# Angle steps and half of the phase tables on GpSimd, kernel rows by DMAs within SBUF

## The reference, cut to what matters

```python
dt = jnp.exp(log_dt)[:, None]                        # 32 groups, 64 states each
mag = jnp.exp(a_re * dt)
ab_re, ab_im = mag * jnp.cos(a_im * dt), mag * jnp.sin(a_im * dt)
inv = 1.0 / (a_re * a_re + a_im * a_im)
g_re = ((ab_re - 1.0) * a_re + ab_im * a_im) * inv
g_im = (ab_im * a_re - (ab_re - 1.0) * a_im) * inv
bb_re, bb_im = g_re[..., None] * b_re - g_im[..., None] * b_im, g_re[..., None] * b_im + g_im[..., None] * b_re
bu_re, bu_im = einsum('blgp,gnp->blgn', ug, bb_re), einsum('blgp,gnp->blgn', ug, bb_im)
# x[t] = ab * x[t-1] + bu[t], complex, over 512 positions
y = einsum('blgn,gpn->blgp', x_re, c_re) - einsum('blgn,gpn->blgp', x_im, c_im) + d * ug
```

## Time and profile before

| | us |
|---|---|
| median of 3 runs (2448.57 to 2450.28) | 2449.53 |
| the profiled execution | 2448.28 |
| its span, first to last instruction | 2446.5 |
| TensorE busy | 2387.8 (98%) |
| VectorE busy | 1469.5 (60%) |
| ScalarE busy | 1080.2 (44%) |
| GpSimd busy | 164.4 (7%) |

### The profile page before, as it was taken

How to read it: one execution, slowest core, us unless ns; L and a number is a source line. 1 busy time by engine, 2 the same in 40 slices (tenths; PEclk the granted TensorE clock), 3 DMA queues, 4 the chain that set the end, 5 groups by cost and what they waited for, 6 DMA issues and landing times.

```text
span 2446.5 us, 33247 instructions
## 1 busy us (share of the span) xinstructions
PE 2387.8 (98%) x11675; PEld 1941.0 (79%) x11675; DVE 1469.5 (60%) x2142; ACT 1080.2 (44%) x1458; POOL 164.4 (7%) x159
## 2 busy tenths in 40 slices
PE   8999999999999999999999999999999989999998
PEld 6767888888788878888887777888888767888887
DVE  7986654532676646455236766887533686687722
ACT  5345433332556644333224644555423473454421
POOL 2011100000100011000002021000011012000000
PEclk9999999999999999999999999999999999999999
DMA  7331233333222222333333102333334202333331
GB/s 175 69 95 52 78 103 94 92 95 100 75 78 77 69 78 86 94 94 99 95 99 93 44 10 86 103 103 94 95 95 125 72 10 61 90 106 94 93 95 64
DMA packets 400952, 209.69 MB, mean 86 GB/s; under 512 B 18131, under 2 KB 397655, under 8 KB 400871
## 3 DMA queue, kind: packets, MB, share of 16 engines
q1 hardware_dynamic: 397111, 199.65, 28.2%
q0 software_dynamic: 3424, 8.91, 1.5%
q10 hardware_dynamic: 336, 0.05, 0.0%
HBM read 204.38 MB, written 4.19 MB: 85 GB/s over the span
## 4 chain that ended last, share of the span: by engine, by line
PE 82%; DVE 12%; ACT 3%; issue 2%; DVEq 1%; DMA 0%; ACTq 0%; SPq 0%
PE bank L677 67%; PE bank L723 4%; DVE tmp L1956 2%; DVE w_lo L1924 2%; PE bank L727 2%; PE bank L1308 1%; DVEq L1953 1%; PE bank L1284 1%; DVE small L2708 1%; PE bank L1259 1%; PE bank L1222 1%; PE bank L1179 0%; ACT w_hi L1382 0%; PE bank L753 0%; PE bank L1118 0%
## 5 line engine op out<-in xcount | busy, mean ns | idle before, releaser
L1924 DVE TENSOR_TENSOR w_lo<-w_raw,w_hi 128x1024 fp32r<-128x1024 f32 x380 | 472.2, 1243 | 540.9 <-ACT w_hi L1382 536.5
L677 PE MATMUL bank<-h_hi,w_hi 128*128 128x512 f32 x1840 | 725.5, 394 | 2.0 <-DVE w_lo L1924 1.0
L677 PE MATMUL bank<-h_lo,w_hi 128*128 128x512 f32 x1840 | 716.8, 390 | 0.0
L677 PE MATMUL bank<-h_hi,w_lo 128*128 128x512 f32 x1840 | 716.1, 389 | 0.0
L1382 ACT ACTIVATE w_hi<-w_raw 128x1024 fp32r<-128x1024 f32 x380 | 402.2, 1059 | 636.7 <-PE bank L677 619.1
L677 PEld LDWEIGHTS bank<-h_hi,w_hi 128*128 128x128 f32 x1840 | 345.6, 188 | 77.0 <-issue 4.0
L677 PEld LDWEIGHTS bank<-h_hi,w_lo 128*128 128x128 f32 x1840 | 345.7, 188 | 72.7 <-issue 2.4
L677 PEld LDWEIGHTS bank<-h_lo,w_hi 128*128 128x128 f32 x1840 | 345.4, 188 | 72.1
L677 PE MATMUL bank<-hid_hi,w_hi 128*128 128x512 f32 x704 | 273.9, 389 | 0.0
L677 PE MATMUL bank<-hid_hi,w_lo 128*128 128x512 f32 x704 | 273.9, 389 | 0.0
L677 PE MATMUL bank<-hid_lo,w_hi 128*128 128x512 f32 x704 | 273.9, 389 | 0.0
(11 more groups left out here) (472 smaller groups left out, 2854.4 us busy)
## 6 DMA issues: line engine op xcount, KB each, us to landing
w_raw<-in_ffn_w SPq DMA_DIRECT2D x120, 512.0 KB, 3.8
w_raw<-in_w_up SPq DMA_DIRECT2D x88, 512.0 KB, 3.7
w_raw<-in_c_w_in SPq DMA_DIRECT2D x32, 512.0 KB, 4.0
w_raw<-in_w_down SPq DMA_DIRECT2D x32, 512.0 KB, 3.6
w_raw<-in_w_in SPq DMA_DIRECT2D x28, 512.0 KB, 3.8
w_raw<-in_w_o SPq DMA_DIRECT2D x16, 512.0 KB, 3.6
w_raw<-in_ab_w_in SPq DMA_DIRECT2D x12, 512.0 KB, 5.8
w_raw<-in_ffn_w SPq DMA_DIRECT2D x16, 384.0 KB, 3.2
```

What stands on the lines that cost most here:

```text
L677: mm = nc.tensor.matmul(out[:], w[:, s, k], v[:, kt], start=(kt == 0 and w is w_hi and v is hi), stop=(kt == sum(slabs) - 1 and v is lo))
L1924: nc.vector.tensor_tensor(w_lo[:, s], w_raw[:, s], w_hi[:, s].bitcast(F32), ALU.subtract).then_inc(lo_done, 1)
```

## The change

Kernel rows: the eight shift matmuls and ScalarE's eight copies are gone. GpSimd issues eight DMAs from `sq_sum`, where `s5_k` lies, to `s5_conv`, each to other partitions, and seven memsets for the partitions in front of them. For that `s5_conv` is laid out with the group innermost, and so is `s5_k`.

Angles: GpSimd computes all eight angle levels (five operations each, three squarings of the first) as soon as VectorE is done with the single angle, into buffers of their own, and VectorE waits for them (`s5_pool`) before its table.

Tables: GpSimd builds the first 16 groups, VectorE the other 16. GpSimd's levels 0 to 3 stand before the store of `us`, level 4 behind it, level 5 behind the eight loads of `u_step`. VectorE waits for GpSimd's half (`s5_pool` at 2) before `turn_and_sum(0)`. TensorE waits for the loads, for the eight kernel DMAs and for the memsets before `enter(0)`.

`s5_c` lies elsewhere, and three semaphores between ScalarE and GpSimd are one (`s5_handed`).

```diff
@@ -231,16 +231,16 @@
-        s5_conv = m("s5_conv", [P, GROUPS, STEP, GW], 56)
+        s5_conv = m("s5_conv", [P, STEP, GW, GROUPS], 56)
-        s5_c = m("s5_c", [P, GROUPS, GW], 80)
+        s5_c = m("s5_c", [P, GROUPS, GW], 14)
-        s5_k = sq_sum[:].rearrange("p (g w) -> p g w", g=GROUPS)
+        s5_k = sq_sum[:].rearrange("p (w g) -> p g w", g=GROUPS)
...
@@ -251,6 +251,8 @@
         s5_ldt = small[:, 152:152 + GROUPS]
         s5_t = tmp[:, 0:2].rearrange("p t n -> p (t n)").rearrange("p (g c) -> p g c", g=GROUPS)
         s5_r8 = place("s5_r8", [P, GROUPS])
+        s5_angles = [(s5_v[:, c], s5_v[:, s]) for c, s in ((9, 8), (0, 1), (2, 3), (4, 5), (6, 7), (10, 11))]
+        angles_free, s5_pool = sem("angles_free"), sem("s5_pool")
         u_step = m("u_step", [P, GROUPS, CH], 16)
         s5_pair = m("s5_pair", [P, 4, 2, GROUPS // 4, CH], 24)
         s5_state, s5_z = s5_pair[:, :, 0], s5_pair[:, :, 1]
...
@@ -619,14 +622,70 @@
                                a["ab_b_if"][0, M_HEADS * v:M_HEADS * v + M_HEADS].unsqueeze(1))\
                     .then_inc(lstm_in, 16)
 
-            pool.wait_ge(us_ready, 1)
+            def angle(out, x0, x1, op):
+                nc.gpsimd.tensor_tensor(out, x0, x1, op).then_inc(pool_part, 1)
+                n(pool_part)
+
+            def angle_settle():
+                pool.wait_ge(pool_part, n.now(pool_part))
+
+            def double_angles():
+                cc, ss, cs = (s5_v[:, j] for j in (12, 13, 14))
+                ec, es = s5_angles[0]
+                for level in (0, 0, 0, 1, 2, 3, 4, 5):
+                    angle(cc, ec, ec, ALU.mult)
+                    angle(ss, es, es, ALU.mult)
+                    angle(cs, ec, es, ALU.mult)
+                    angle_settle()
+                    ec, es = s5_angles[level]
+                    angle(ec, cc, ss, ALU.subtract)
+                    angle(es, cs, cs, ALU.add)
+                    angle_settle()
+                pool.drain().then_inc(s5_pool, 1)
+
+            def double_table(level):
+                m_, half = 1 << level, slice(0, GROUPS // 2)
+                ec, es = (t[:, half].unsqueeze(2).to_broadcast([P, GROUPS // 2, m_]) for t in s5_angles[level])
+                c0, s0, c1, s1 = (t[:, half, k] for t, k in ((s5_cos, slice(0, m_)), (s5_sin, slice(0, m_)),
+                                                            (s5_cos, slice(m_, 2 * m_)), (s5_sin, slice(m_, 2 * m_))))
+                t0 = s5_t[:, half, 0:m_]
+                angle(c1, c0, ec, ALU.mult)
+                angle(t0, s0, es, ALU.mult)
+                angle(s1, c0, es, ALU.mult)
+                angle_settle()
+                angle(c1, c1, t0, ALU.subtract)
+                angle_settle()
+                angle(t0, s0, ec, ALU.mult)
+                angle_settle()
+                angle(s1, s1, t0, ALU.add)
+                angle_settle()
+
+            pool.wait_ge(angles_free, 1)
+            double_angles()
+            pool.wait_ge(prep["vector_to_pe"], 1)
+            for t, value in ((s5_cos, 1.0), (s5_sin, 0.0)):
+                nc.gpsimd.memset(t[:, 0:GROUPS // 2, 0:1], value).then_inc(pool_part, 1)
+                n(pool_part)
+            angle_settle()
+            for level in range(4):
+                double_table(level)
+            pool.wait_ge(s5_handed, 1)
             pool.dma_start(us_dram.rearrange("(k p) i c -> p k i c", p=P), us[:]).then_inc(us_stored, 16)
+            double_table(4)
             pool.wait_ge(us_stored, 16)
             by_step = us_dram.rearrange("(g p) i c -> i p g c", p=GW)
             for i in range(STEP):
                 k = STEP - 1 - i
                 pool.dma_start(u_step[GW * k:GW * k + GW], by_step[i]).then_inc(us_loaded, 16)
-            pool.wait_ge(ys_ready, 1)
+            double_table(5)
+            pool.drain().then_inc(s5_pool, 1)
+            pool.wait_ge(s5_handed, 2)
+            for j in range(STEP):
+                r = GW * (STEP - 1 - j)
+                pool.dma_start(s5_conv[r:P, j].rearrange("p w g -> p (w g)"), sq_sum[0:P - r]).then_inc(s5_conv_in, 16)
+            for j in range(STEP - 1):
+                nc.gpsimd.memset(s5_conv[0:GW * (STEP - 1 - j), j], 0.0).then_inc(s5_pool, 1)
+            pool.wait_ge(s5_handed, 3)
             by_step = ys_dram.rearrange("(g p) j c -> j p g c", p=GW)
             for j in range(STEP):
                 pool.dma_start(by_step[j], ys_step[GW * j:GW * j + GW]).then_inc(ys_stored, 16)
...
@@ -872,12 +931,6 @@
 
                 product(h_hi, h_lo, [KD], 1, each=kernels)
                 product(h_hi, h_lo, [KD], 1)
-                pe.wait_ge(prep["scalar_to_pe"], n(prep["scalar_to_pe"]))
-                for j in range(STEP):
-                    out = take(5 + j % 3)
-                    off = P - GW * (STEP - 1 - j)
-                    nc.tensor.matmul(out[:], shifted[:, off:off + P], s5_k.rearrange("p g w -> p (g w)"),
-                                     start=True, stop=True).then_inc(prep["pe_to_scalar"], 1)
 
             def s5_core():
 
...
@@ -908,13 +961,15 @@
                     pe.wait_ge(s5["vector_to_pe"], n(s5["vector_to_pe"]))
                     for g in range(8):
                         c = g * CH
-                        nc.tensor.matmul(out[:, c:c + CH], s5_conv[:, 8 * i + g].rearrange("p j w -> p (j w)"),
+                        nc.tensor.matmul(out[:, c:c + CH], s5_conv[:].rearrange("p j w g -> p (j w) g")[:, :, 8 * i + g],
                                          u_step[:, 8 * i + g], start=True, stop=False)
                         mm = nc.tensor.matmul(out[:, c + 1:c + CH], s5_out[:, 8 * i + g].rearrange("p j w -> p (j w)"),
                                               s5_state[:, i, g, 0:CH - 1], start=False, stop=True)
                     mm.then_inc(s5["pe_to_scalar"], 1)
 
                 pe.wait_ge(us_loaded, 16 * STEP)
+                pe.wait_ge(s5_conv_in, 16 * STEP)
+                pe.wait_ge(s5_pool, 2 + STEP - 1)
                 enter(0)
                 enter(1)
                 swap_inputs(0)
...
@@ -1500,23 +1555,19 @@
                         outputs()
                     if t == 1:
                         columns()
-                act.drain().then_inc(us_ready, 1)
+                act.drain().then_inc(s5_handed, 1)
                 for i in range(GROUPS // 4):
                     act.wait_ge(prep["pe_to_scalar"], n(prep["pe_to_scalar"]))
                     nc.scalar.activation(s5_in[:, 4 * i:4 * i + 4], bank[4 + i % 4][:].rearrange("p (g w) -> p g w", g=4),
                                          ACT.Copy).then_inc(bank_free[4 + i % 4], 1)
                 act.wait_ge(prep["pe_to_scalar"], n(prep["pe_to_scalar"]))
                 nc.scalar.activation(s5_k, bank[4][:].rearrange("p (g w) -> p g w", g=GROUPS), ACT.Copy)\
-                    .then_inc(prep["scalar_to_pe"], 1)
+                    .then_inc(s5_handed, 1)
                 act.drain().then_inc(bank_free[4], 1)
                 act.wait_ge(prep["vector_to_scalar"], n(prep["vector_to_scalar"]))
 
                 for t in (0, 1):
                     gate_in(t)
-                for j in range(STEP):
-                    act.wait_ge(prep["pe_to_scalar"], n(prep["pe_to_scalar"]))
-                    nc.scalar.activation(s5_conv[:, :, j], bank[5 + j % 3][:].rearrange("p (g w) -> p g w", g=GROUPS),
-                                         ACT.Copy).then_inc(bank_free[5 + j % 3], 1)
 
             def convolved(tiles):
                 for k in tiles:
...
@@ -2115,6 +2166,7 @@
                 step(nc.vector.tensor_copy(re[:, 1], v[10]))
                 step(nc.vector.tensor_copy(im[:, 1], v[11]))
                 settle()
+                nc.vector.tensor_scalar(v[8], v[8], sign, -1.0, ALU.mult, ALU.mult).then_inc(angles_free, 1)
                 for m_ in (1, 2, 4):
                     def last(t):
                         return t[:, m_:m_ + 1].to_broadcast([P, m_, GROUPS])
...
@@ -2165,45 +2217,29 @@
                     settle()
                 flag(prep["vector_to_scalar"])
 
-                ec, es, t2, t3 = v[9], v[8], v[12], v[13]
-
-                def square():
-                    tt(t2, ec, ec, ALU.mult)
-                    tt(t3, es, es, ALU.mult)
-                    stt(es, ec, 2.0, es, ALU.mult, ALU.mult)
-                    settle()
-                    tt(ec, t2, t3, ALU.subtract)
-                    settle()
-
-                for _ in range(3):
-                    square()
-                ts(es, es, sign, -1.0, ALU.mult, ALU.mult)
-                step(nc.vector.memset(s5_cos[:, :, 0:1], 1.0))
-                step(nc.vector.memset(s5_sin[:, :, 0:1], 0.0))
-                settle()
-                m_ = 1
-                while m_ < CH:
-                    def by(t):
-                        return t.unsqueeze(2).to_broadcast([P, GROUPS, m_])
-
-                    c0, s0, c1, s1 = (t[:, :, k] for t, k in ((s5_cos, slice(0, m_)), (s5_sin, slice(0, m_)),
```

(34 more changed lines are left out.)

## The result

The changed kernel takes **2489.5 us** (median of four runs, 2487.9 to 2492.1), the kernel before 2449.9 beside it. The ratio is 1.0163, 95% interval 1.0147 to 1.0179, so the change makes the kernel slower, by 1.6%. The profiled execution took 2489.08 us with a span of 2487.3, 40.8 above the span before. The forecast was 2481.1 with a range of 2448 to 2500: it holds the time, and the likeliest case names the right order of events, but the sizes of its terms were off in both directions. One execution among those of the first experiment was slow (2678.4 us, mean granted clock 0.844), and it is left out.

A forecast was written before the change was run, and what follows sets the result against it. VectorE's list was taken as the bound from 35.83 to 149.49 us, with TensorE's full too. +31.3 (late enter(0)) and +0.3 (leave) on 2448.28 gave 2479.9, with 1.25 for the median 2481.1 us; range 2448 to 2500.

The forecast's parts named there:

- the likeliest case: GpSimd and VectorE take turns, one short GpSimd instruction per VectorE instruction, delaying enter(0): +31.6 us, 2481.1 us, chance 0.42.
- GpSimd between VectorE's instructions: While VectorE builds its matrices, one waiting GpSimd instruction gets in at each boundary; angles end at about 87 us.
- A: Rival: GpSimd's short instructions slip between VectorE's at no cost; angles end at 49, -3.1 us, 2446.4 us, chance 0.21.
- B: Rival: several short GpSimd instructions per VectorE boundary; angles end at 66, +14.4 + 0.3 us, 2464.2 us, chance 0.20.
- The size of the collision: In the angle steps: VectorE pushed by 38 x 0.17 = 6.5 us to 87.0, angles ready at about 87 instead of 49.
- C: As rival: strided weights slow in leave, +7.0 us, 2488.1 us, chance 0.17. As a time: end of level 5, forecast 122.3.
- C + 8.8: Start of enter(0): eighth kernel DMA issued 4.4 us after level 5's end at C, landing 4.4 us later.
- T: Time at which TensorE starts enter(0): 97.06 us in the kernel before, forecast 131.1 us after the change.
- T - 99.8: What the change is worth in us, from when enter(0) starts; nothing changes at 99.8; forecast +31.3.
- Clock: TensorE idle for 41 us before enter(0): nothing taken for the granted clock afterwards, up to 11 us kept for the upper end.
- Layout: Strided s5_conv weight loads in leave taken as free, other end 7.0 us; leave's lost cover adds 0.3 us.
- 9.6 us the most: Largest possible gain: shift matmuls gone and no other wait, so enter(0) starts at 90.20 us, -9.6 us.

The follow-up runs named there:

- the first experiment: The kernel before with only the strided layout of s5_conv and the kernel row, group innermost; 2460.4 us, ratio 1.0043.
- the second: The changed kernel whole, but leave reads 128 neighbouring columns of s5_conv, so wrong numbers in the same amount of work; 2478.1 us, ratio 1.0107.
- the fourth experiment: The changed kernel without GpSimd's two drains, the flags standing on the last instructions instead; 2485.5 us, ratio 1.0142.

## Why the prediction held, and where it didn't

*GpSimd between VectorE's instructions.* Right in kind. Three angle steps take 3.57 us and the next two 2.43 behind VectorE's 1024-column instructions, some 1.2 us each. From 45.6 to 76.0 us there are 25 steps beside 25 VectorE instructions: one GpSimd instruction per VectorE instruction. That excludes A (49 us) and B (66). With VectorE idle the forty steps and their waits take 9.96 us, not 8.1. The first memsets (0.13 and 0.12 us at 78.03, beside a VectorE split) and the DMA issues (5.04 us for eight) kept their own length, as forecast.

*The size of the collision.* This is the term that was mis-sized, in two ways. I counted 8 to 10 angle steps into VectorE's small operations before 45 us, which left some 30 for its long ones. The trace has 15 there, in 4.3 us, and 25 left: about 7 us. And I let VectorE pay 0.17 us for each GpSimd instruction that got in. In its long instructions it pays next to nothing: its output matrix ends at 81.9, 1.4 us later than before and not 6.5, and about half of that arose in the small operations before 45.5. That is the other 4 us. So the angles end at 76.0 instead of 87, eleven us early, and C is 109.75, not 122.3. VectorE does pay where its instructions are as short as GpSimd's: in its table those of 256 columns take up to 0.84 us, where 0.42 is usual before. That is hidden here, as TensorE waits for GpSimd.

*The tail behind level 5.* C + 8.8 was short: T - C is 12.7 us. The drain, counted as nothing, takes 4.03 of it. The landing (4.26 for the last) and the memsets (3.31 / 7 = 0.47 each) were as estimated.

*Together*, T = 122.4, not 131.1: +22.6 us by T - 99.8. Removing the drains gave 4.0 us back, and moving the wait 9.1. Moving the wait is a way out that I didn't see: I listed what TensorE awaits ahead of `enter(0)` and never asked whether `enter` reads it.

*Clock.* I took nothing, with up to 11 us at the upper end. It costs 4.4 us, as the filled wait shows: `turn_back(0)` at T + 27.3, not T + 23.0. The cost isn't the same each time. In the profiled executions of the second and the fourth experiment, in which this stage is unchanged, `turn_back(0)` comes at T + 29.6 and T + 30.1.

*Layout.* I took nothing and gave C 0.17. C's mechanism is real, shown alone and in the change. In the strided kernel with rows by DMA one of the 32 groups of `leave` starts 0.655 us after the one before it at full clock:
```profile
132.09 0.54 PE L936 MATMUL bank<-u_step,s_conv 128*128 128x64 f32 x2
...
132.69 0.59 PE L936 MATMUL bank<-u_step,s_conv 128*128 128x64 f32 x2
```
and in its twin with neighbouring columns 0.447:
```profile
134.17 0.39 PE L936 MATMUL bank<-u_step,s_conv 128*128 128x64 f32 x2
...
134.62 0.39 PE L936 MATMUL bank<-u_step,s_conv 128*128 128x64 f32 x2
```
(means over 7 and 30 groups, from 132.69 and 134.17 on). That is 32 x 0.208 = 6.7 us if the clock held, near C's 7.0. What I had no case for is the second half: the clock falls, a group then takes 0.853 (by the rows from 140 us on), and with the gates behind it the layout costs 11.1 to 11.4 us. Why the clock falls under these loads no run shows. The Trainium skill ("SBUF — State Buffer", section Door 1) says that each access that goes to another 16-byte line pays. For TensorE's weights the runs agree (192 ns to 304, both at full clock). The row that I set against it doesn't speak to it. VectorE's instruction at 45.98 reads each power 16 times over and moves 32 elements on only then, while a weight load moves on at each column. Its unchanged 1.22 us were no evidence for a free stride on either engine, and with them falls the reason that I gave for C's smaller chance. None of the rows shown has VectorE read with that step at each column.

*The account.* +22.6 (T), +4.4 (clock after the idle time) and +11.4 (layout) make +38.4 of the measured 39.6 (2489.5 - 2449.9). The forecast of +31.6 came near it by luck: a T that was 8.7 us too late stood in for 15.8 us of clock and layout.

*What the change could have brought.* I called 9.6 us the most. The angles alone bring 3.1 (2449.2 to 2446.1), and with no layout cost, no late rows and the clock held the whole of the remaining idea brings the same 3.1. In that kernel VectorE starts its first sum at 103.92, straight from its table, 4.2 us after the first swap is done (98.61 + 1.08); TensorE's 7.03 us are slack there. A VectorE table that is itself shortened on top of this wasn't tried. Nor was an unstrided layout with right values, which the rows' DMAs don't write.

## What to carry to other kernels

Before a wait is placed, ask which instruction reads what it waits for: one wait moved past code that reads nothing of it gave back 9.1 of 39.6 us. Price an idle stretch of TensorE with the clock behind it; here a wait of 4.9 us cost 2.8 us more in waits of VectorE behind it, and 20 small matmuls removed them. A layout that saves work for its writer is to be priced at its reader, on the reader's own engine and with its own order of reads: which index runs innermost decides whether a row with "the same stride" says anything.

## What the runs showed of the hardware

- Granted clock falls under strided weight loads though the rows show TensorE busy throughout: from 1.00 to 0.50, 4 to 6 us into `leave`, in all eight kernels with them, in none of the six whose `leave` read neighbouring columns.
- A weight load of columns 32 elements apart took 304 ns at full clock and 327 at half, one of neighbouring columns 192 to 197 and 333.
- From `enter(0)` to `swap_sums` 21.6 to 22.1 us passed where the clock was held. Behind an idle stretch at half clock it was 26.2 to 26.5 us in the profiled executions of five kernels and 28.3 to 28.9 in four.
- Where VectorE and GpSimd collided, VectorE with long instructions back to back lost almost nothing (1.22 to at most 1.28 us), GpSimd with short dependent ones 25 of 35 us.
- A GpSimd drain behind its own DMAs stands until about 0.5 us after the last has landed: 4.03 us in the changed kernel, where the last load landed 3.6 us after level 5's end, and 0.79 in the kernel with TensorE kept busy, where it landed 0.2 us after it.
- Transfers within SBUF queued right behind 1 MB of loads landed in 6.4 to 11.5 us in five kernels, and in 1.8 to 4.3 us in the changed kernel, where the loads had landed first.
